# Gate and up of five feed-forward parts: one 512-column product for the high weight, halves added on VectorE

## The reference

```python
def _swiglu(h, w_gate, w_up, w_down):
    return (jax.nn.silu(h @ w_gate) * (h @ w_up)) @ w_down

for layer in range(DEPTH):                       # second block, DEPTH = 2
    h = _rmsnorm(x, ffn1_norm[layer])
    x = x + 0.5 * _swiglu(h, ffn1_w_gate[layer], ffn1_w_up[layer], ffn1_w_down[layer])
    ...                                          # a mixer
    h = _rmsnorm(x, ffn2_norm[layer])
    x = x + 0.5 * _swiglu(h, ffn2_w_gate[layer], ffn2_w_up[layer], ffn2_w_down[layer])
```

## Time and profile before

| what | value |
|---|---|
| time, median of 3 runs | 2057.93 us (2055.55 to 2061.33) |
| span of the profiled execution | 2055.0 us, the profile gives no other time for it |
| mean granted TensorE clock | 0.908 of full speed |
| TensorE busy | 1822.3 us, 89% |
| VectorE busy | 1172.8 us, 57% |
| ScalarE busy | 767.7 us, 37% |
| GpSimd busy | 208.0 us, 10% |
| chain of waits that ended last, by engine | PE 71%, DVE 16%, DMA 5%, ACT 4%, issue 3% |
| on it, L1550 (gate, up and others) and L1575 (down and others) | 37% and 18% |

### The profile page before, as it was taken

The page is one execution under the profiler, slowest core; times in us unless marked ns, Lnnn a source line. Parts: engine busy times, 40 slices in busy tenths (PEclk is TensorE's granted clock), DMA queues, the critical chain, the costliest instruction groups (busy, mean ns, idle before and its releaser), DMA issues.

```text
span 2055.0 us, 29152 instructions
## 1 busy us (share of the span) xinstructions
PE 1822.3 (89%) x11650; PEld 1629.2 (79%) x11650; DVE 1172.8 (57%) x1423; ACT 767.7 (37%) x908; POOL 208.0 (10%) x228
## 2 busy tenths in 40 slices
PE   3889799989997999699989577899989998789998
PEld 2787599978876999599889433799979998678997
DVE  5884577767645444648546598444444444434443
ACT  1443334334433443333344300433343334334442
POOL 2000000100000000199200022000000000300000
PEclk9995899999857999899999668999999999879999
DMA  8880468954602555354553100355535554314552
GB/s 292 312 318 1 144 211 292 329 190 157 232 15 92 183 187 187 120 168 163 181 166 125 60 21 0 128 184 184 184 123 184 184 184 144 123 53 133 186 186 96
DMA packets 221336, 329.87 MB, mean 161 GB/s; under 512 B 6265, under 2 KB 183002, under 8 KB 221282
## 3 DMA queue, kind: packets, MB, share of 16 engines
q1 hardware_dynamic: 205896, 276.85, 40.4%
q0 software_dynamic: 14832, 52.12, 7.2%
q10 hardware_dynamic: 554, 0.17, 0.0%
HBM read 328.03 MB, written 1.09 MB: 160 GB/s over the span
## 4 chain that ended last, share of the span: by engine, by line
PE 71%; DVE 16%; DMA 5%; ACT 4%; issue 3%; DVEq 0%; POOLq 0%; SPq 0%; POOL 0%; ACTq 0%
PE bank L1550 37%; PE bank L1575 18%; DMA s_late<-in_w_ada 4%; DVE s_late L1145 4%; PE bank L1561 4%; DVE s_wL L1128 2%; PE bank L1665 1%; ACT s_wH L843 1%; PE bank L1657 1%; PE bank L1656 1%; PE bank L1601 1%; DVE s_hL L1163 1%; DVE s_mix L524 1%; DMA s_raw<-in_w_ffn_in 1%; PE bank L1677 1%
## 5 line engine op out<-in xcount | busy, mean ns | idle before, releaser
L1128 DVE TENSOR_TENSOR s_wL<-s_raw,s_wH 128x2048 fp32r<-128x2048 f32 x254 | 601.6, 2375 | 496.4 <-ACT s_wH L843 496.0
L1550 PE MATMUL bank<-s_hH,s_wH 128*128 128x256 f32 x2496 | 711.3, 285 | 2.3 <-ACT s_mix L912 1.2
L1550 PE MATMUL bank<-s_hL,s_wH 128*128 128x256 f32 x2496 | 707.5, 283 | 0.0
L1550 PE MATMUL bank<-s_hH,s_wL 128*128 128x256 f32 x2496 | 707.4, 283 | 0.0
L843 ACT ACTIVATE s_wH<-s_raw 128x2048 fp32r<-128x2048 f32 x254 | 484.4, 1908 | 253.7 <-PE bank L1575 231.8
L1550 PEld LDWEIGHTS bank<-s_hH,s_wH 128*128 128x128 f32 x2496 | 480.4, 192 | 9.4 <-issue 4.6
L1550 PEld LDWEIGHTS bank<-s_hL,s_wH 128*128 128x128 f32 x2496 | 480.4, 192 | 3.1 <-issue 0.5
L1550 PEld LDWEIGHTS bank<-s_hH,s_wL 128*128 128x128 f32 x2496 | 480.1, 192 | 0.0
L1575 PE MATMUL bank<-s_wH,s_aH 128*128 128x512 f32 x528 | 209.5, 397 | 18.3 <-DVE s_aL L1261 18.3
L1575 PE MATMUL bank<-s_wL,s_aH 128*128 128x512 f32 x528 | 208.2, 394 | 0.0
L1575 PE MATMUL bank<-s_wH,s_aL 128*128 128x512 f32 x528 | 207.6, 393 | 0.0
(11 more groups left out here) (337 smaller groups left out, 1882.3 us busy)
## 6 DMA issues: line engine op xcount, KB each, us to landing
s_raw<-in_w_ffn_in SPq DMA_DIRECT2D x44, 1024.0 KB, 5.1
s_raw<-in_ffn_w_gate SPq DMA_DIRECT2D x44, 1024.0 KB, 5.2
s_raw<-in_ffn_w_up SPq DMA_DIRECT2D x44, 1024.0 KB, 5.1
s_raw<-in_ffn_w_down SPq DMA_DIRECT2D x44, 1024.0 KB, 4.7
s_late<-in_w_ada POOLq DMA_DIRECT2D x20, 2048.0 KB, 9.7
s_raw<-in_w_ffn_out SPq DMA_DIRECT2D x22, 1024.0 KB, 4.8
s_raw<-in_w_in_ab SPq DMA_DIRECT2D x12, 1024.0 KB, 10.2
s_raw<-in_w_in_cd SPq DMA_DIRECT2D x12, 1024.0 KB, 7.9
```

Source lines behind the costliest of these rows:

```text
L1128: TTn(wL[:, slot, :], raw[:, slot, :], wH[:, slot, :].bitcast(F32), ALU.subtract).then_inc(lo_ready, 1)
L1550: last = mm(dst[:, ft * T:ft * T + T], w, h[:, k, :], start=(k == 0 and i == 0), stop=(k == KC - 1 and i == 2))
```

## The change

In five of the six parts (all but `ff0`) `cols_unit` is replaced by `wide_unit` for gate and up. `hH` and `hL` become two halves of one tile `hX`, so that one product takes the high weight tile against both: 512 columns, of which the first 256 of the bank receive high x high and the last 256 high x low. The low weight tile against `hH` is added to the first 256. A unit now has 16 products of 512 and 16 of 256 columns in place of 48 of 256. Its two column halves go to two banks: gate to 4 and 5, up to 6 and 7. VectorE then adds the halves of each bank (`joined`): two copies of the last 256 columns of the two banks to SBUF (`gate_up`), a wait for these (`g_first`, `u_first`), two additions of the first 256, and `g_sum` or `u_sum`. ScalarE's silu waits for `g_sum` and reads SBUF, and so does the multiplication for up. TensorE waits for `g_sum` before the next gate unit, where it waited for silu. In VectorE's order the gate's join stands at the head of a round, ahead of the two splits, and up's join ahead of the multiplication.

```diff
--- before.py
+++ after.py
@@ -48,6 +48,8 @@
 SUMS = {n: i for i, n in enumerate(["o_ab", "ff0", "o_cd", "ff1", "f1a", "o_even", "f2a", "f1b", "o_odd", "f2b"])}
 FFN = {n: i for i, n in enumerate(["ff0", "ff1", "f1a", "f2a", "f1b", "f2b"])}
 
+WIDE = {n: i for i, n in enumerate(["ff1", "f1a", "f2a", "f1b", "f2b"])}
+
 LO0 = USED0 = EVAC0 = 3
 
 
@@ -99,8 +101,8 @@
         wL = sb("wL", [P, RING, UNIT], F32R)
         x = sb("x", [P, TT, D])
         t32 = sb("t32", [P, KC, T])
-        hH = sb("hH", [P, KC, T], F32R)
-        hL = sb("hL", [P, KC, T], F32R)
+        hX = sb("hX", [P, 2, KC, T], F32R)
+        hH, hL = hX[:, 0], hX[:, 1]
         mix = sb("mix", [P, 10368])
         aH = sb("aH", [P, 2, T], F32R)
         aL = sb("aL", [P, 2, T], F32R)
@@ -143,6 +145,7 @@
 
         sil = carve(mix, 0, 512)
         act = carve(mix, 512, 512)
+        gate_up = {n: carve(mix, 4096 if n == "ff1" else 1024, 2, 512) for n in WIDE}
 
         ada_raw = carve(late, 0, 2, KC * 512)
         ada_acc = carve(late, 8192, 2, 512)
@@ -168,6 +171,7 @@
             sem(s) for s in ("nat_ready", "tr_done", "t32_ready", "t32_odd", "th_ready", "tl_ready"))
         y_first = sem("y_first")
         sil_done, act_mul, act_hi, act_lo = (sem(s) for s in ("sil_done", "act_mul", "act_hi", "act_lo"))
+        g_first, g_sum, u_first, u_sum = (sem(s) for s in ("g_first", "g_sum", "u_first", "u_sum"))
         flip_mm, flip_out = sem("flip_mm"), sem("flip_out")
         s_ready, s_max, p_ready, pT_ready, pT_copied, o_ready, o_done = (
             sem(s) for s in ("s_ready", "s_max", "p_ready", "pT_ready", "pT_copied", "o_ready", "o_done"))
@@ -943,7 +947,11 @@
 
                 def silu(i):
                     act_e.wait_ge(act_mul, i + f) if not (isinstance(i, int) and i + f == 0) else None
-                    A(sil, bank[4][:], ACT.Silu).then_inc(sil_done, 1)
+                    if name in WIDE:
+                        act_e.wait_ge(g_sum, i + (11 * WIDE[name] + 1))
+                        A(sil, gate_up[name][:, 0, :], ACT.Silu).then_inc(sil_done, 1)
+                    else:
+                        A(sil, bank[4][:], ACT.Silu).then_inc(sil_done, 1)
 
                 act_e.wait_ge(unit_used, n0 + USED0 + 1)
                 silu(0)
@@ -1254,23 +1262,54 @@
             def ffn(name, with_ada=False):
                 n0, f = START[name], 11 * FFN[name]
 
+                w = 11 * WIDE[name] if name in WIDE else 0
+
+                def joined(i, part, b, first, done):
+
+                    dst = gate_up[name][:, part, :]
+                    for ft in range(2):
+                        at = slice(ft * T, ft * T + T)
+                        last = dve.tensor_copy(dst[:, at], bank[b + ft][:, T:2 * T])
+                    last.then_inc(first, 1)
+                    dve.wait_ge(first, i + (w + 1))
+                    for ft in range(2):
+                        at = slice(ft * T, ft * T + T)
+                        last = TTn(dst[:, at], dst[:, at], bank[b + ft][:, 0:T], ALU.add)
+                    last.then_inc(done, 1)
+
+                def gate(i, n):
+
+                    if name in WIDE:
+                        dve.wait_ge(unit_used, n + (USED0 + 1))
+                        joined(i, 0, 4, g_first, g_sum)
+
                 def hidden(i, n, slot):
 
-                    TTn(act, sil, bank[5][:], ALU.mult).then_inc(act_mul, 1)
+                    up = bank[5][:]
+                    if name in WIDE:
+                        joined(i, 1, 6, u_first, u_sum)
+                        dve.wait_ge(u_sum, i + (w + 1))
+                        dve.wait_ge(sil_done, i + (f + 1))
+                        up = gate_up[name][:, 1, :]
+                    TTn(act, sil, up, ALU.mult).then_inc(act_mul, 1)
                     dve.wait_ge(act_hi, i + (f + 1))
                     TTn(aL[:], act.rearrange("p (a t) -> p a t", a=2), aH[:].bitcast(F32), ALU.subtract).then_inc(act_lo, 1)
                     split(slot, n)
 
+                gate(0, n0)
                 split_py(n0 + 3)
-                dve.wait_ge(sil_done, f + 1)
+                if name not in WIDE:
+                    dve.wait_ge(sil_done, f + 1)
                 dve.wait_ge(unit_used, n0 + USED0 + 2)
                 hidden(0, n0 + 4, (n0 + 4) % RING)
 
                 def body(i):
                     n = i * 3 + (n0 - 1)
+                    gate(i, n)
                     split((n0 + 5) % RING, n + 3)
                     split((n0 + 6) % RING, n + 4)
-                    dve.wait_ge(sil_done, i + (f + 1))
+                    if name not in WIDE:
+                        dve.wait_ge(sil_done, i + (f + 1))
                     dve.wait_ge(unit_used, n + (USED0 + 3))
                     hidden(i, n + 5, (n0 + 7) % RING)
 
@@ -1551,6 +1590,16 @@
                                       stop=(k == KC - 1 and i == 2))
                 last.then_inc(unit_used, 1)
 
+            def wide_unit(slot, n, b):
+
+                H, L = unit_in(slot, n)
+                for ft in range(2):
+                    for k in range(KC):
+                        wh, wl = H[:, k, ft * P:ft * P + P], L[:, k, ft * P:ft * P + P]
+                        mm(bank[b + ft][:], wh, hX[:, :, k, :], start=(k == 0), stop=False, skip_group_check=True)
+                        last = mm(bank[b + ft][:, 0:T], wl, hH[:, k, :], start=False, stop=(k == KC - 1), skip_group_check=True)
+                last.then_inc(unit_used, 1)
+
             def toks_unit(slot, n, dst):
 
                 H, L = unit_in(slot, n)
@@ -1695,16 +1744,32 @@
                 n0, f = START[name], 11 * FFN[name]
                 for b in range(4):
                     mm(bank[b][:], zeros[:, 0:128], zeros[:, 128:640], start=True, stop=False, skip_group_check=True)
-                cols_unit(n0 % RING, n0, bank[4])
-                cols_unit((n0 + 1) % RING, n0 + 1, bank[5])
+
+                def gate(slot, n):
+                    if name in WIDE:
+                        wide_unit(slot, n, 4)
+                    else:
+                        cols_unit(slot, n, bank[4])
+
+                def up(slot, n):
+                    if name in WIDE:
+                        wide_unit(slot, n, 6)
+                    else:
+                        cols_unit(slot, n, bank[5])
+
+                gate(n0 % RING, n0)
+                up((n0 + 1) % RING, n0 + 1)
 
                 def body(i):
                     n = i * 3 + (n0 - 1)
-                    pe.wait_ge(sil_done, i + f)
-                    cols_unit((n0 + 2) % RING, n, bank[4])
+                    if name in WIDE:
+                        pe.wait_ge(g_sum, i + 11 * WIDE[name])
+                    else:
+                        pe.wait_ge(sil_done, i + f)
+                    gate((n0 + 2) % RING, n)
                     pe.wait_ge(act_lo, i + f)
                     rows_unit((n0 + 3) % RING, n + 1, aH, aL, 0, False, False)
-                    cols_unit((n0 + 4) % RING, n + 2, bank[5])
+                    up((n0 + 4) % RING, n + 2)
 
                 if with_ada:
                     with pe.Fori(0, 2) as m:
```

## The result

The change makes the kernel slower: 2069.86 us median of 20 runs, against 2055.56 us of the kernel before on the same chip; the ratio is 1.0076, with a 95% interval of 1.0055 to 1.0097 (11 to 20 us). The forecast was 2053.8 us, the range 2043 to 2068: wrong in direction, and the median lies outside the range.

A forecast was written before the change was run, and what follows sets the result against it. The prediction took the rounds to be bound by TensorE's rate of products. Its terms, -20.9 + 7.9 + 5.2 + 3.7 = -4.1 us, took 2057.93 to 2053.8 us, with a range of 2043 to 2068.

The forecast's parts named there:

- Removed on TensorE: Gate and up units: one 512 and one 256 product replace three of 256, 11.9 ns less a pair, -20.9 us.
- Rival 4: Two-piece 512 product pays its fixed part again at the seam, decided under 6 ns saved; 2074.7 us, chance 0.10.
- The clock at the ends: Longer idle gaps ending the five parts lower TensorE's clock, slowing the down unit behind: +5.2 us, at most 5.9.
- The join, J: VectorE's two copies and two additions a unit take 1.57 us, uncovered in five end gaps: +7.9 us.
- Steady rounds: Joins hide beside TensorE's work: VectorE's round 15.78 us, TensorE's 16.60, so J may rise to 1.98 us.
- rival 3: VectorE becomes the bound in steady rounds if J passes 1.98 us; some 2079 us at J = 2.2; chance 0.10.
- f1a: In the part where GpSimd works beside VectorE, joins add to TensorE's wait for aL: +3.7 us, bounds 0 and 10.
- Rival 1: At the part ends gaps cost only J, the clock holds and f1a absorbs the joins: 2044.9 us, chance 0.20.

The follow-up runs named there:

- e3: Changed kernel with the two halves of hX interleaved by chunk, so the wide product's moving operand is one piece of 512; 2081.88 us, ratio 1.0116.
- e8: Changed kernel with each column half's eight wide products first, then its eight narrow ones; ratio 1.0042 against the kernel before.
- e1: Changed kernel with 14 products of zeros on TensorE in the idle gap ending each of the five parts; 2058.76 us, ratio 1.0016.
- e5: Kernel before, old products kept, with VectorE's joins added as copies and a maximum of each half with itself; 2075.39 us, ratio 1.0112.
- e2: Changed kernel with the last up unit of each part made the old way, so no join in the end gap; 2059.24 us, ratio 1.0003.
- e4: Changed kernel without the joins, halves not added, so output is not the reference's; 2052.25 us, ratio 0.9961.
- e7: Changed kernel with f1a made the old way, the other four parts wide; 2063.18 us, ratio 1.0039.
- e10: Kernel before with eight products of zeros in the end gap of the same five parts; 2055.3 us, ratio 0.9968.
- e11: Changed kernel, wide products grouped, f1a the old way, last up units narrow, eight products of zeros in all five end gaps; 2041.5 us, ratio 0.991.
- e6: Changed kernel with ScalarE making the high part of unit n+3 ahead of silu in the wide parts; ratio 1.0106.
- e9: Changed kernel with wide products before narrow ones in each column half and 14 products of zeros in the end gaps; 2059.47 us, ratio 0.999.

## Why the prediction was wrong

The direction turned on two terms of the sum; the others came out near their size, one of them in part by luck.

- **Removed on TensorE: mis-sized.** Forecast -20.9 us (11.9 ns a pair). Measured -12.3 for the units (6.9 ns a pair, 352.8 ns) and -10.8 with the down units. The step that failed is "The nearest is the plain 512-column product, and I take it": both rows came from stretches in which every product has the same width. In alternation the wide one takes 235.9 and the narrow one 116.9 ns. Rival 4 gave the wrong place for such a loss: e3 excludes the seam. By the prediction's own mark, less than 6 ns saved a pair, it was not rival 4 either, but it came close. Grouped (e8), the round has 16.61 us where 16.60 was forecast. The rule "N / 2.4 + 2.5 ns" of the Trainium skill, "TensorE: Matmul & The Clock Gate", section "Back-to-back issue gap", is not borne out by any order measured here: 119 to 120 ns and 228 to 230 ns in equal widths. The section itself calls that the spacing of an isolated product; of its limits the prediction told only that weight loads set the spacing too.
- **The clock at the ends: mis-sized by half.** Forecast +5.2 us ("four times 1.48 us = 5.9 at most"). Measured +10.5 in the profile, and e1 takes some 12 us away with it. The step that failed was to take the one low row behind a gap of 2.23 us as the upper bound behind one of 3.8 us (4.02 from start to start): four ends of the changed kernel lose 2.3 to 2.7 us, and `f1a`, which the forecast left out as slow already, loses 1.2 more than before. The size of a loss goes with the clock in the gap: of the 29 gaps of 4.0 us, 15 had a clock of 0.93 to 1.00 and lost 1.3 to 1.7 us behind them, all five of e5 and four of e8 among them; 14 had 0.78 to 0.90, so the clock was down for part of the gap already, and lost 2.3 to 2.8. What decides when it falls is not settled. One of five was also a poor measure of the kernel before: e2 and e4 show that a fall is uncertain already at 2.5 us, and the same trace holds a second slow end, that of `ff0` (columns as in the earlier trace rows):

```profile
447.37:454.71 7.34, 7.34 (x24) 5.58 (x24) 5.99 (x12) 2.50 (x3) 0.00 (x0) 0.77 0.51 161
```

- **The join, J: right.** 1516.45 - 1514.87 = 1.58 us on the chain, 1.57 forecast; +7.5 us at the ends against +7.9.
- **Steady rounds: right.** VectorE kept pace with 2J in the round (e5: 16.98 us exactly), so rival 3 did not come about. The timeline of the changed kernel shows how near it was: up's join at 1602.90 starts 1.19 us after VectorE became free.

```profile
1602.90 0.76 DVE L1272 COPY s_mix<-bank 128x256 f32<-128x256 f32 x2 [1.19 <-PE bank L1600]
1603.69 0.75 DVE L1277 TENSOR_TENSOR s_mix<-s_mix,bank 128x256 f32<-128x256 f32 x2
1604.57 0.69 DVE L1294 TENSOR_TENSOR s_mix<-s_mix 128x512 f32<-128x512 f32 x1
1605.96 0.69 DVE L1296 TENSOR_TENSOR s_aL<-s_mix,s_aH 128x512 fp32r<-128x512 f32 x1 [0.70 <-ACT s_aH L946]
1607.77 2.29 DVE L1136 TENSOR_TENSOR s_wL<-s_raw,s_wH 128x2048 fp32r<-128x2048 f32 x1 [1.12 <-ACT s_wH L847]
1609.98 0.75 DVE L1272 COPY s_mix<-bank 128x256 f32<-128x256 f32 x2
```

- **f1a: near in size, incomplete in reason.** +3.7 us of waits forecast and, between the two profiles, measured; that they agree to the tenth is luck. The rounds of `f1a` lose 3.5 to 8.9 us in the four profiles with `f1a` the old way (before, e7, e10, e11), and 12.6 to 15.1 in seven of the eight with the joins (19.9 in e3). Part of the reasoning holds: the joins are not stretched, and VectorE's splits take 6.9 us less in all (94.3 to 87.4). But the prediction overlooked that the multiplication loses its bank operand: the eleven take 11.0 us in place of 7.5. How much of TensorE's wait is due to the joins and how much to the multiplication was not separated; e6 shows only that the order of silu and the high part does not matter. The Trainium skill says in "SBUF — State Buffer", section "Who interferes with whom", that a VectorE instruction with two inputs in SBUF contends with a GpSimd instruction that reads SBUF, and that the ports that they share are an exclusive lock. The trace agrees: 3.36 us against 0.67, and each of these long ones ends 0.55 us after the GpSimd instruction beside which it started.
- **The sum** with measured terms: -10.8 + 7.5 + 10.5 + 3.7 + 1.1 = +12.0 us for the five parts, in one pair of profiles; the ratio gives +15.6 (11 to 20) for the whole kernel. Rival 1 (the clock holds) is excluded by the windows of the changed kernel. No rival had the two mis-sized terms together; with the first of them right the five parts would have come out at +2 us, with the second at +7.
- **Range and chances.** The range ended 1.9 us below the result, since its upper end was set half-way into rival 4 and not from the clock term, which I had bounded at 5.9 us.

## What to carry to other kernels

A product's price taken from a stretch of equal products may not hold when two widths alternate; put equal ones together, or measure the pair in the order in which it will run. Work that hides in every steady round still has to be paid where the loop ends, and there a longer idle time of TensorE may cost twice, once itself and once by the clock; some products of zeros in that gap are a cheap test of it, and here a gain even for the kernel before. When an operand moves from a bank to SBUF, ask whether GpSimd works on SBUF at that time.

## What the runs showed of the hardware

- In alternation a 512-column fp32r product takes 235.9 ns to the next start and a 256-column one 116.9 (changed kernel, e3), in groups of eight some 230 and 119 ns (e8); in alternation it is the same with the moving operand in one piece or two. Why alternation costs 5 ns a pair is not known.
- At a granted clock of 0.50 products of 256 columns start every 0.21 to 0.22 us, which is 256 columns at 1.2 GHz and no more; at 1.00 the line through 119.9 and 227.9 ns leaves 12 ns a product beside the columns.
- With gaps of 2.44 to 2.67 us (start to start) in the dense work of TensorE the clock fell in 14 of 29 cases, for 1.4 to 1.6 us of loss each; with 4.0 us in 29 of 29, for 1.3 to 2.8 us; with products of zeros in the gap in none of twenty (e1, e9, e10, e11).
- Beside GpSimd's table work a VectorE instruction of 128x512 with both operands in SBUF takes up to 4.2 us (e3) where it takes 0.69 alone. Each of the 40 that take over 1.3 us in `f1a` ends 0.55 us after the GpSimd instruction that ran when it started. With an operand in a bank the multiplication keeps its 0.67 to 0.69 us (before, e4, e7, e10, e11).
- Executions of one kernel on one core ranged over 28 us (before, 2040 to 2068). In the profiles the steady rounds are the same to 0.01 us wherever the products have the same form and order; what differs is the clock, the ends and `f1a`.
